# A hand-written order of attention steps among projection steps is replaced in a hybrid encoder layer

## What is computed

```
u = rmsnorm(h)
z = u @ w_in            # [A q | A k | A v | B q | B k | B v]
mixer A: 8 heads x 64, chunk-band attention with a learned bias by clipped distance
mixer B: 8 heads; p1 - lambda * p2 of two softmax maps mixes 128-wide values, ALiBi,
         block-causal mask, then per-head RMSNorm
g_A, g_B = sigmoid(u @ w_gate)
h += rmsnorm((g_A * (oA @ w_branch_a) + g_B * (oB @ w_branch_b)) @ w_out)
h += rmsnorm(relu(rmsnorm(h) @ w_up)^2 @ w_down)
h += sigmoid(h @ w_ple_gate) * rmsnorm(p @ w_ple)
```

## Time and profile before

| | us |
|---|---|
| median of 3 runs | 1137.86 |
| their range | 1137.24 to 1138.68 |
| the profiled execution's own time | 1138.13 |
| span in its trace, first to last instruction | 1136.6 |
| TensorE busy (8252 matmuls) | 1100.1 (97%) |
| VectorE busy | 601.7 (53%) |
| ScalarE busy | 509.2 (45%) |
| GpSimd busy | 524.1 (46%) |
| DMA, share of its 16 engines (hardware queue) | 29.3% |
| granted TensorE clock, mean | 0.99 |

### The profile page before, as it was taken

One profiled execution on the slowest core, in us unless ns is written; L12 is line 12 of the kernel. 1 busy time (PEld: TensorE's weight loads), 2 busy tenths in 40 slices (PEclk: granted clock), 3 DMA queues, 4 the chain that ended last, 5 costly groups with the idle time before them and its releaser, 6 DMA issues.

```text
span 1136.6 us, 22594 instructions
## 1 busy us (share of the span) xinstructions
PE 1100.1 (97%) x8252; PEld 1054.6 (93%) x8252; DVE 601.7 (53%) x1200; ACT 509.2 (45%) x1103; POOL 524.1 (46%) x432
## 2 busy tenths in 40 slices
PE   9799999999999999999999999989999999999898
PEld 7799899999899889999999989989999999999897
DVE  4556766767555651112442657886515713732755
ACT  6255455555455553332232563336524622652652
POOL 3555555565544433334445544434534434344541
PEclk9899999999999999999999999999999999999999
DMA  8134533343134322232222212223322332232123
GB/s 182 57 96 100 127 89 84 95 106 95 58 96 105 96 68 84 82 100 79 83 84 81 69 47 75 86 64 101 94 83 85 89 88 83 76 104 82 56 76 84
DMA packets 219617, 99.14 MB, mean 87 GB/s; under 512 B 62785, under 2 KB 216634, under 8 KB 219538
## 3 DMA queue, kind: packets, MB, share of 16 engines
q1 hardware_dynamic: 214098, 88.74, 29.3%
q0 software_dynamic: 5440, 9.34, 2.5%
HBM read 88.57 MB, written 11.02 MB: 88 GB/s over the span
## 4 chain that ended last, share of the span: by engine, by line
PE 62%; issue 19%; POOL 9%; DVE 6%; ACT 2%; DMA 1%; POOLq 0%; SPq 0%; DVEq 0%; ACTq 0%
PE proj L1745 44%; POOL w_lo L570 9%; PE score L1868 3%; PE proj L2057 2%; PE turn_out L1928 2%; PE turn_out L1958 2%; PE turn_out L1950 1%; PE proj L2144 1%; PE turn_out L1955 1%; PE score L1880 1%; PE proj L2018 1%; PE proj L1825 1%; PE turn_out L1903 1%; DMA x_tm<-x_prompt 1%; DVE sq_sum L1437 1%
## 5 line engine op out<-in xcount | busy, mean ns | idle before, releaser
L570 POOL TENSOR_TENSOR w_lo<-w_raw,w_hi 128x512 fp32r<-128x512 f32 x292 | 387.3, 1334 | 483.7 <-ACT w_hi L753 483.3
L753 ACT ACTIVATE w_hi<-w_raw 128x512 fp32r<-128x512 f32 x292 | 180.5, 627 | 284.6 <-PE proj L1745 252.8
L1745 PE MATMUL proj<-act_hi,w_hi 128*128 128x288 f32 x1088 | 246.8, 308 | 0.8 <-ACT wide L995 0.3
L1745 PE MATMUL proj<-act_lo,w_hi 128*128 128x288 f32 x1088 | 233.9, 297 | 0.0
L1745 PE MATMUL proj<-act_hi,w_lo 128*128 128x288 f32 x1088 | 233.3, 296 | 0.0
L1745 PEld LDWEIGHTS proj<-act_hi,w_hi 128*128 128x128 f32 x1088 | 172.8, 190 | 12.9 <-issue 7.8
L1745 PEld LDWEIGHTS proj<-act_hi,w_lo 128*128 128x128 f32 x1088 | 175.7, 189 | 0.0
L1745 PEld LDWEIGHTS proj<-act_lo,w_hi 128*128 128x128 f32 x1088 | 175.7, 189 | 0.0
L1745 PE MATMUL proj<-mid_hi,w_hi 128*128 128x288 f32 x608 | 131.8, 298 | 5.5 <-DVE wide L1568 4.1
L1745 PE MATMUL proj<-mid_hi,w_lo 128*128 128x288 f32 x608 | 131.0, 296 | 0.0
L1745 PE MATMUL proj<-mid_lo,w_hi 128*128 128x288 f32 x608 | 130.8, 296 | 0.0
(11 more groups left out here) (311 smaller groups left out, 2113.7 us busy)
## 6 DMA issues: line engine op xcount, KB each, us to landing
w_raw<-w_in SPq DMA_DIRECT2D x72, 256.0 KB, 3.2
w_raw<-w_up SPq DMA_DIRECT2D x64, 256.0 KB, 2.9
w_raw<-w_down SPq DMA_DIRECT2D x64, 256.0 KB, 2.8
w_raw<-w_gate SPq DMA_DIRECT2D x32, 256.0 KB, 2.8
w_raw<-w_branch_b SPq DMA_DIRECT2D x16, 256.0 KB, 2.8
w_raw<-w_out SPq DMA_DIRECT2D x16, 256.0 KB, 2.8
w_raw<-w_ple_gate SPq DMA_DIRECT2D x16, 256.0 KB, 2.8
out<-k_out SPq DMA_DIRECT2D x48, 64.0 KB, 1.9
```

Of the source, the lines that this page charges most:

```text
L570: pool.tensor_tensor(w_lo[:, slot], w_raw[:, slot], w_hi[:, slot].bitcast(F32), ALU.subtract).then_inc(lo_done, 1)
L753: act.activation(w_hi[:, slot], w_raw[:, slot], ACT.Copy).then_inc(hi_done, 1)
L1745: last = pe.matmul(out[:, h], w[:, slot, at], x[:, k, HALF * h:HALF * h + HALF], start=(k == 0 and s == 0), stop=(k == blocks - 1 and s == 2))
```

## The change

It changes the order of instructions and nothing that is computed.

1. Both lists of steps are written anew. Shown here are their first lines; the rest is given by what the paragraphs below say.
2. Ahead of the first unit GpSimd makes two w_lo, then k_lo and q_lo, then four w_lo; VectorE writes vT before it pads q.
3. o_r is made at CK or V4, whichever comes first in the list; before, always at V4.
4. The four DMAs of the band table go one by one to the start of the third to the sixth unit.

```
-B_STEPS = [("V4", 0, 0), ("S", 0, 0), ("C", 0, 3), ("CK", 0, 0), ("S", 1, 0), ("T", (0, 0), 3), ("S", 2, 0),
+B_STEPS = [("S", 0, 0), ("V4", 0, 4), ("C", 0, 0), ("S", 1, 0), ("T", (0, 0), 3), ("CK", 0, 0), ("C", 1, 0),
...
-            for n in range(4):
+            for n in range(2):
                 lo_part(Count(RING + n))
             for n in range(2):
                 lo_of_kq(Count(0), n, 0)
-            for n in range(4, 6):
+            for n in range(2, 6):
                 lo_part(Count(RING + n))
...
+                rooted = prev != "B"
                 for name, arg, t in walk(steps, prev == "B"):
+                    if not rooted and name in ("CK", "V4"):
+
+                        at_least(pool, o_summed, u)
+                        pool.tensor_tensor(o_r[:, :], o_ms[:, 1 - par], neg_half[:, :], ALU.pow).then_inc(o_rooted, 1)
+                        rooted = True
...
-                    elif name == "V4" and prev == "B":
-
-                        at_least(pool, o_summed, u)
-                        pool.tensor_tensor(o_r[:, :], o_ms[:, 1 - par], neg_half[:, :], ALU.pow).then_inc(o_rooted, 1)
...
+            def spread_band(n):
+
+                rows_, row = band[bass.ds(n, 2)], band_row[bass.ds(n, 2)]
+                pool.dma_start(rows_, row.unsqueeze(1).broadcast_to([2, P, BW])).then_inc(band_kept, 16)
+
             pool.wait_ge(band_row_kept, 16)
-            for u in range(NA):
-                pool.dma_start(band[2 * u:2 * u + 2], band_row[2 * u:2 * u + 2].unsqueeze(1).broadcast_to([2, P, BW])
-                               ).then_inc(band_kept, 16)
             with pool.Fori(0, (NB - 4) // 2) as it:
                 for v in range(2):
+                    spread_band(Count(2 * v, [(it, 4)]).value())
                     b_unit(Count(2 + v, [(it, 2)]), v)
...
+            projected(Count(0), 2)
             pad_q(Count(0))
-            projected(Count(0), 2)
```

More of the change, by code:

```diff
@@ L36 @@
 PIECE = 512
-A_STEPS = [("S", 0, 0), ("N", (0, 0), 0), ("N", (0, 1), 0), ("CK", 0, 0), ("V4", 0, 4), ("S", 1, 0), ("T", (0, 0), 2),
[5 rows of a table removed]
-B_STEPS = [("V4", 0, 0), ("S", 0, 0), ("C", 0, 3), ("CK", 0, 0), ("S", 1, 0), ("T", (0, 0), 3), ("S", 2, 0),
[3 rows of a table removed]
+A_STEPS = [("S", 0, 0), ("N", (0, 0), 1), ("V4", 0, 0), ("S", 1, 0), ("N", (0, 1), 0), ("N", (1, 0), 0),
[5 rows of a table added]
+B_STEPS = [("S", 0, 0), ("V4", 0, 4), ("C", 0, 0), ("S", 1, 0), ("T", (0, 0), 3), ("CK", 0, 0), ("C", 1, 0),
[3 rows of a table added]
 def walk(steps, with_outputs):
```

## The result

| | before | after |
|---|---|---|
| median of 4 runs each, us | 1137.55 | 1151.61 |
| their range | 1135.59 to 1138.68 | 1147.69 to 1152.05 |
| ratio, with its 95% interval | | 1.0118 (1.0092 to 1.0144) |
| profiled execution, span | 1136.6 | 1149.8 |
| granted TensorE clock, mean | 0.990 | 0.984 |

A forecast was written before the change was run, and what follows sets the result against it. TensorE, busy 97% of the span, was taken as the bound, with at most some 16 us idle to win. -8.4 - 2.5 - 2.8 + 0.7 + 3.9 + 1.1 - 1.0 = -9.0 us, from 1137.9 to 1128.9 us (1122.5 to 1135).

The forecast's parts named there:

- Place 1: First unit: the wait for vT and the half clock behind it go, casts may cost 0.3; -8.4 us.
- Place 2: Third unit: band table DMAs spread over four units; 3.3 us won, 0.8 given back, -2.5 us.
- Place 4: K4 moved late delays a weight piece and S1's bias: +0.7 us over seven kind B units, +3.9 in kind A.
- Place 3: Attention units: 28 fewer runs of steps k, 0.1 us saved at each restart; -2.8 us.
- Place 5: First unit of kind A: waits before S1 and OT plus low clock, +1.1 us; third unit of kind A -1.0.
- rival (c): The late piece costs kind B too, 1 us in each of seven units: 1135 us; chance 0.11.
- (d): Kind B: normalising held through w_lo and k_lo, OT 2.2 us late, 15.4 in seven units: 1144 us; chance 0.07.
- (b): First unit keeps 3 to 4 us of its wait, in VectorE's casts instead of vT: 1132 us; chance 0.12.
- ScalarE's last w_hi released by a DMA of w_raw: Sign for Place 4 in the profile after: a unit's last w_hi waits for its weight piece; otherwise the forecast is wrong.
- units of kind B at 29.9 to 30.4: Sign for Place 2 in the profile after: all kind B units within 0.5 us of each other.

The follow-up runs named there:

- e3_ab_old: The changed kernel with the old step orders of kinds A and B, keeping the start's edits and spread band tables; 1129.94 us, ratio 0.9935.
- e7_s0_first: e3_ab_old with S0 and three steps k put ahead of V4 in kind B; 1123.44 us, ratio 0.9873.
- e6: The changed kernel with K4 early and T(1,0) two steps k later in kind B, and the old order of kind A; 1119.62 us.
- e12: e6 with OT of kind A two steps k later; 1122.50 us, ratio 0.9868.
- f2_sp_a_old: e10_sp_later with the old order of kind A; 1122.10 us, ratio 0.9872.
- e5_k4_early: The changed kernel with K4 alone moved forward, from behind the 18th step k to the 11th (kind B) and 9th (kind A); 1121.66 us.
- e9_k4_b_only: The changed kernel with K4 early in kind B alone, still behind the 18th step k in kind A; 1126.91 us, ratio 0.9921.
- e10_sp_later: The changed kernel, K4 still late, with SyncE's block that waits for K4 one weight piece later; 1121.94 us, ratio 0.9868.
- f1_short_w_lo: The changed kernel, K4 late, with one w_lo per kind B unit cut to 128 of 512 columns (projection partly wrong); 1133.11 us.
- e4_t10_later: The changed kernel with two steps k moved from ahead of OT to ahead of AV0 and T(1,0) in kind B; 1138.23 us.

## Why the prediction was wrong, point by point

**Place 1, the first unit: right.** Forecast -8.4. Its end moved from 77.3 to 70.2 in the changed kernel, and to 67.7 to 70.6 in the others with this order. That spread is older than the unit: the projection ahead of it ended at 37.8 to 40.6 us from run to run. From its last step to the last AV4 it is 38.2 us before, 35.0 in e3_ab_old, 31.1 in e7_s0_first and 30.0 in every kernel with the changed order of kind B: 8.2 won. So the edits of GpSimd and VectorE alone give less than half (e3_ab_old still waits 2.8 us for vT), and S0 and steps k ahead of V4 most of the rest. The wait for vT and the half clock of the earlier trace rows are gone. S1 waits 0.6 us for its bias behind the casts (forecast 0.3). Two readings on the way were off and cancelled, which is luck: VectorE wrote vT at 42.5 and not at 39.2 to 40.4, since its work on tab_b and lambda stood ahead of it, and the casts then took 1.6 us and not 2.2 to 3.4.

**Place 2, the band tables: right beside the old order.** Forecast -2.5. In e3_ab_old the third unit lost 2.8 us, and no other of kind B grew. The 0.8 given back for a VectorE caught by GpSimd's later chain was not seen there; beside the changed order it may be part of what place 4 brought.

**Place 3, fewer switches: the size near, the mechanism not borne out.** Forecast -2.8. Without waits a unit of kind B takes 29.84 where it took 30.24, kind A 30.82 against 31.07, in all some -4. But the seventh unit of e7_s0_first, with the old eleven runs of k and S0 ahead of V4, is as short. It stands here behind the same unit of e3_ab_old, which has V4 ahead of S0:

```profile
226.06:256.32 30.26, 30.26 (x231) 28.03 (x230) 20.33 (x54) 16.40 (x46) 18.31 (x17) 1.00 0.42 108
220.76:250.63 29.87, 29.87 (x233) 27.93 (x231) 20.21 (x54) 16.40 (x46) 18.36 (x17) 1.00 0.44 109
```

So 0.39 of the 0.4 come with S0 ahead of V4, which the prediction did not price, and 0.03 are left for three restarts: 0.01 each, where I took 0.1. That the total came near is luck. Most other units of e7_s0_first lost 0.2 to 0.5 us more from T(2,0) on: VectorE's C2, caught by GpSimd's w_lo and k_lo, took 1.5 + 0.6 us there and 0.2 + 1.7 in the seventh.

**Place 5: near.** Forecast +1.1 for the first unit of kind A. S1 waited 2.28 us (forecast 1.7; 1.32 with K4 early) and OT 2.31 (2.8); the unit took 34.9 to 37.6 with K4 early, against 36.0. The third unit lost its 1.04, but it lost it with the old order of kind A too, in e6, e7 and e12, and kept it in e3_ab_old and f2_sp_a_old. So the new order is not shown to be the reason.

**Place 4, K4 late: here it failed.** I had +4.6, and undoing K4's place alone (e5_k4_early) gave 30.0. The step that failed is the +0.7 for the seven units of kind B, where e5_k4_early measured 20.8. Of the 29.2 us between the two profiled executions 20.8 stand in the seven units of kind B and 5.6 in kind A; 1.5 stand in the projection ahead of the first unit and 1.2 behind the units, where K4 has no part. The mechanism that I named was right up to the bias: K4, six us of SyncE, the piece, the last w_hi, the squares, the bias, S1. In kind A the biases of the next S0 ended 3.1 to 3.6 us behind its start (forecast 3.1 into the unit), and S1 waited 1.3 to 1.8 us (1.3); e9_k4_b_only prices kind A at 5.3 (3.9). Three things were wrong in kind B.

1. The margin in front of S1 was taken too wide. My own terms, 27.7 + 2.7 to 4.0 + 2.8 - 30.2, make 3.0 to 4.3 and not 3.6 to 4.4, in a unit of the old length. The piece took 4.05 and 4.2 us to land, above the rows' 2.7 to 4.0, and the unit without waits is 0.4 shorter. So the bias ended 4.6 to 5.6 us behind S0 in the seven units, and S1, due at 4.4, waited 0.2 to 1.2 us in six of them, 3.4 in all where I had 0.7. These waits feed themselves: in e10_sp_later, the same order without them, K4 ended 21.8 us into its unit, as reckoned (21.7), and in the changed kernel not before 23.0. This is rival (c), to which I gave 0.11, with about its price: in f1_short_w_lo, where T(1,0) does not wait, the seven units took 0.9 us each more than in e5_k4_early.
2. I followed the late piece on ScalarE and VectorE and left out GpSimd, though its w_lo stands in the same sentence of the code. The w_lo of the late piece, the load of cv, tab_b, the next w_lo and o_r stand in one row on GpSimd, and the w_lo beside C1 moved by 2.6 to 3.4 us in the second to the seventh unit, by 1.2 in the eighth. The prediction had both halves in hand: place 2 was priced by a C1 held by GpSimd, and (d) asked whether another VectorE instruction would be held. Neither asked it for C1 in the new order, where AV0 and T(1,0) no longer had two steps k each behind S2. The waits there are 9.4 us.
3. The clock. I counted its fall for place 1 and place 5, but not for the waits that place 4 brings. Over the seven units kind B lost 20.8 us against e5_k4_early: 9.4 at T(1,0), 3.6 at S1 and a later score step, and 7.8 are left. Of these 6.6 stand in the three units with a stretch at half clock, where the granted clock was 0.79 over 110 to 118, 0.57 over 146 to 154 and 0.66 over 214 to 219. TensorE's busy time there times what is missing to 1.00 makes 6.2 us (an estimate), so nearly all of the 6.6 is the clock.

**The sum without place 4** would have been -13.6, 1124.3; e5_k4_early took 1121.7. So the sum of the other places held within 3 us, place 3 in it by luck, and the miss comes with one moved step of an engine off the critical path. Whether it would be as large without the spread tables is open.

**The rivals.** (d) did not come: OT waits nowhere in kind B of the changed kernel (in e4_t10_later it does, 0.6 to 0.7 us in four units). But it was the right kind of question, a VectorE instruction caught behind GpSimd's w_lo, at the wrong instruction. "S1's bias in the first unit" (b) was small. Of what I named as proof, "ScalarE's last w_hi released by a DMA of w_raw" was there, ten times; "units of kind B at 29.9 to 30.4" was not.

**The rule that I cited.** The Trainium skill (SBUF — State Buffer, Who interferes with whom) says who issues first holds the port for its whole instruction. The trace agrees on which side loses: c_map, begun 0.12 us behind a w_lo, was held. It does not agree on how long: that w_lo ended at 143.98, and c_map at 145.10, with the end of the o_r behind it. By the rule it would have been through some 0.9 us earlier (an estimate: its 0.22 us behind 143.98). So the measurement decides.

## What to carry to other kernels

A step that no one near it waits for is not free to move: ask what is queued behind it on the queue that waits for it (here a weight piece behind eight stores), and follow what comes late through every engine that handles it, not only along the one that you first think of. If a transfer has to wait for a late step, let the urgent one go first in the queue; one condition in SyncE's list was worth as much here as moving K4 in both orders. And a new wait of 1 to 3 us on TensorE is to be priced with what the clock may take behind it: in kind B of the changed kernel 13.0 us of waits came with 7.8 more, and in e4_t10_later, where the longest wait of kind B was 1.32, no half clock came.
